# Retention's keys regrouped: 0 to 127, 128 to 255 and the last 16, in place of 16, 128 and 128

## The reference, cut to what matters

```
sc = jnp.einsum('bhid,bhjd->bhij', qc, kc) * intra          # decay gamma^|n-m|
o = (jnp.einsum('bhij,bhjv->bhiv', sc, vc)
     + jnp.einsum('bhid,bhdv->bhiv', qc * q_dec[:, :, None], S))
S = S * chunk_dec[:, None, None] + jnp.einsum('bhjd,bhjv->bhdv', kc * k_dec[:, :, None], vc)
```

## Time and profile before

| | |
|---|---|
| median of three runs | 1411.36 us (1410.07 to 1412.16) |
| the profiled execution | 1412.0 us, its span 1409.1 us |
| TensorE busy | 1385.0 us, 98% |
| VectorE, ScalarE, GpSimd busy | 1012.6, 697.2, 283.7 us |
| granted TensorE clock, mean | 0.996 |

### The profile page before, as it was taken

The page is one execution under the profiler, slowest core; times in us unless marked ns, Lnnn a source line. Parts: engine busy times, 40 slices in busy tenths (PEclk is TensorE's granted clock), DMA queues, the critical chain, the costliest instruction groups (busy, mean ns, idle before and its releaser), DMA issues.

```text
span 1409.1 us, 25044 instructions
## 1 busy us (share of the span) xinstructions
PE 1385.0 (98%) x10088; PEld 1321.5 (94%) x10088; DVE 1012.6 (72%) x1591; ACT 697.2 (49%) x1131; POOL 283.7 (20%) x273
## 2 busy tenths in 40 slices
PE   7999999999999999999999999999999999999997
PEld 7989999999999888889999999999999999888887
DVE  5668766655786988788666776766557785898864
ACT  5556544443654555544334564544444555555542
POOL 1014100022144100032244554000024402200021
PEclk9999999999999999999999999999999999999999
DMA  7424556655432755555444354555555552365552
GB/s 237 150 91 150 180 163 195 190 183 175 150 121 90 227 182 181 178 181 187 143 140 141 128 179 159 174 178 180 165 166 160 161 180 90 121 209 192 189 168 80
DMA packets 225482, 229.45 MB, mean 163 GB/s; under 512 B 13576, under 2 KB 218632, under 8 KB 225368
## 3 DMA queue, kind: packets, MB, share of 16 engines
q1 hardware_dynamic: 224432, 225.98, 49.9%
q10 hardware_dynamic: 936, 1.87, 0.6%
HBM read 226.51 MB, written 1.33 MB: 162 GB/s over the span
## 4 chain that ended last, share of the span: by engine, by line
PE 91%; DVE 5%; ACT 1%; issue 1%; POOL 0%; DMA 0%; POOLq 0%; DVEq 0%; ACTq 0%
PE ps L500 27%; PE ps L498 19%; PE ps L499 19%; PE ps L495 16%; DVE ul L1464 1%; PE ps L736 1%; PE ps L810 1%; PE ps L578 1%; PE ps L548 1%; PE ps L550 1%; PE ps L549 1%; PE ps L572 1%; PE ps L800 1%; PE ps L646 1%; PE ps L725 1%
## 5 line engine op out<-in xcount | busy, mean ns | idle before, releaser
L970 ACT ACTIVATE uh<-raw 128x1024 fp32r<-128x1024 f32 (+4 forms) x455 | 447.8, 993 | 466.7 <-PE ps L500 422.8
L1464 DVE TENSOR_TENSOR ul<-raw,uh 128x1024 fp32r<-128x1024 f32 (+4 forms) x455 | 534.2, 1180 | 141.5 <-PE ps L500 107.3
L500 PE MATMUL ps<-xx,ul 128*128 128x272 f32 (+1 forms) x2160 | 618.4, 286 | 0.0
L498 PE MATMUL ps<-xx,uh 128*128 128x272 f32 (+1 forms) x1456 | 430.3, 296 | 0.9 <-DVE ul L1464 0.8
L499 PE MATMUL ps<-xx,uh 128*128 128x272 f32 (+1 forms) x1456 | 418.6, 287 | 0.0
L500 PEld LDWEIGHTS ps<-xx,ul 128*128 128x128 f32 x2160 | 406.8, 188 | 0.1
L500 PE MATMUL ps<-aa,ul 128*128 128x272 f32 (+1 forms) x1104 | 315.4, 286 | 0.0
L498 PEld LDWEIGHTS ps<-xx,uh 128*128 128x128 f32 x1456 | 274.8, 189 | 5.3 <-issue 2.6
L499 PEld LDWEIGHTS ps<-xx,uh 128*128 128x128 f32 x1456 | 275.2, 189 | 1.2
L495 PE MATMUL ps<-xx,uh 128*128 128x512 f32 x704 | 248.5, 395 | 1.9 <-DVE ul L1464 1.1
L498 PE MATMUL ps<-aa,uh 128*128 128x272 f32 (+1 forms) x840 | 245.4, 292 | 2.9 <-ACT aa L1109 2.7
(11 more groups left out here) (256 smaller groups left out, 1386.4 us busy)
## 6 DMA issues: line engine op xcount, KB each, us to landing
raw<-in_ffn_w SPq DMA_DIRECT2D x60, 1024.0 KB, 5.2
raw<-in_ffn_w_in SPq DMA_DIRECT2D x44, 1024.0 KB, 5.2
raw<-in_ret_w_in SPq DMA_DIRECT2D x24, 1024.0 KB, 5.2
raw<-in_ffn_w_out SPq DMA_DIRECT2D x16, 1024.0 KB, 5.4
raw<-in_gla_w_in SPq DMA_DIRECT2D x12, 1024.0 KB, 5.6
raw<-in_ret_w_o SPq DMA_DIRECT2D x8, 1024.0 KB, 5.2
raw<-in_dsa_w_in SPq DMA_DIRECT2D x7, 1024.0 KB, 5.2
raw<-in_ffn_w_out SPq DMA_DIRECT2D x8, 768.0 KB, 4.9
```

What stands on the lines that cost most here:

```text
L498: e.matmul(ps[:, 0:n1 - n0], hi[:, k, :], x.hi[:, k0 + j, n0:n1], start=first and j == 0, stop=False)
L500: i = e.matmul(ps[:, 0:n1 - n0], lo[:, k, :], x.hi[:, k0 + j, n0:n1], start=False, stop=last and j == len(ks) - 1)
L970: i = e.activation(unit_hi(u)[:, :, cols], a, ACT.Copy)
L1464: i = e.tensor_tensor(unit_lo(u)[:, :, cols], a, unit_hi(u)[:, :, cols].bitcast(F32), ALU.subtract)
```

## The change

The 16 keys that stand alone move from the front to the end. The groups become keys 0 to 127 with 272 queries, 128 to 255 with the 192 queries from 80 on, and 256 to 271 with the 64 queries from 208 on. In all three kinds of matmul the small group is now taken at its true size: 16 stationary columns in the scores and the transposes, 16 stationary rows in the outputs. The second and third groups of scores share one bank and one step (r = 1), so that `scores` has two parts. VectorE multiplies them in two instructions. The memset and its semaphore fall away. The decay tables are 528 columns wide.

```diff
-NI = (272, 256, 128)
-I0 = (0, 16, 144)
-DOFF = (0, 272, 528)
-DW = 656
+RKEY = (0, 128, 256)
+RSIZE = (128, 128, 16)
+NI = (272, 192, 64)
+I0 = (0, 80, 208)
+DOFF = (0, 272, 464)
+DW = 528
...
             def ret_v(c):
-                to_tokens(("rv", c), tmp[4 + c % 2], *lin.emptied(("rv", c)))
-
-            def scores(hd, g):
-                ps = small(("rS", hd, g), "D")
+                ps = small(("rv", c), "A")
+                w.wait_ge(*lin.emptied(("rv", c)))
+                for g in range(3):
+                    i = e.transpose(ps[0:RSIZE[g], g * P:(g + 1) * P], tmp[4 + c % 2][:, RKEY[g]:RKEY[g] + RSIZE[g]], ident)
+                done(i, ("rv", c))
+
+            def scores(hd, part):
+
+                ps = small(("rS", hd, part), "D")
                 w.wait_ge(s_rrope, 4 * hd + 4)
-                for k in range(2):
-                    i = e.matmul(ps[:, 0:NI[g]], r_kq[:, 2 * hd + k, WIN[g]:WIN[g] + P], r_kq[:, 8 + 2 * hd + k, I0[g]:T],
-                                 start=(k == 0), stop=(k == 1))
-                done(i, ("rS", hd, g))
+                for g in (range(1), range(1, 3))[part]:
+                    to = ps[0:RSIZE[g], DOFF[g] - DOFF[part]:DOFF[g] - DOFF[part] + NI[g]]
+                    for k in range(2):
+                        i = e.matmul(to, r_kq[:, 2 * hd + k, RKEY[g]:RKEY[g] + RSIZE[g]], r_kq[:, 8 + 2 * hd + k, I0[g]:T],
+                                     start=(k == 0), stop=(k == 1))
+                done(i, ("rS", hd, part))
...
                 for g in range(3):
-                    i = e.matmul(ps[:, I0[g]:T], r_vt[:, g, c * P:(c + 1) * P], r_sc[hd % 2][:, DOFF[g]:DOFF[g] + NI[g]],
+                    keys = slice(0, RSIZE[g])
+                    i = e.matmul(ps[:, I0[g]:T], r_vt[keys, g, c * P:(c + 1) * P], r_sc[hd % 2][keys, DOFF[g]:DOFF[g] + NI[g]],
                                  start=(g == 0), stop=(g == 2))
...
-                    if r < 3:
+                    if r < 2:
                         scores(hd, r)
...
             def ret_v(c):
-                to_tokens(("rv", c), r_vt[:, :, c * P:(c + 1) * P], s_rzero, 1)
+                key, dst = ("rv", c), r_vt[:, :, c * P:(c + 1) * P]
+                ps = aux.bank(key)
+                w.wait_ge(*aux.full(key))
+                e.activation(dst[0:RSIZE[2], 2, :], ps[0:RSIZE[2], 2 * P:3 * P], ACT.Copy)
+                e.activation(dst[:, 0:2, :], ps[:, 0:2 * P].rearrange("p (a b) -> p a b", a=2), ACT.Copy).then_inc(
+                    aux.empties(key, "A"), 1)
...
-                        e.tensor_tensor(r_sc[hd % 2][:, cols], aux.bank(key)[:, 0:NI[r]], r_dk[hd % 2][:, cols],
-                                        ALU.mult).then_inc(aux.empties(key, "D"), 1)
+                        for g in (range(1), range(1, 3))[r]:
+                            cols, keys = slice(DOFF[g], DOFF[g] + NI[g]), slice(0, RSIZE[g])
+                            ps = aux.bank(key)[keys, DOFF[g] - DOFF[r]:DOFF[g] - DOFF[r] + NI[g]]
+                            i = e.tensor_tensor(r_sc[hd % 2][keys, cols], ps, r_dk[hd % 2][keys, cols], ALU.mult)
+                        i.then_inc(aux.empties(key, "D"), 1)
...
-            e.memset(r_vt[:, 0, :], 0.0).then_inc(s_rzero, 1)
```

More of the change, by code:

```diff
@@ L442, in build @@
                              "s_acc", "s_best", "s_mask", "s_bm", "s_dmax", "s_dexp", "s_drc", "s_dp", "s_dyh"))
-        (s_rstage, s_rzero, s_metah, s_metasq, s_metal, s_both, s_jr, s_rms, s_fin, s_rcs, s_rrope, s_rsum, s_rsub,
+        (s_rstage, s_metah, s_metasq, s_metal, s_both, s_jr, s_rms, s_fin, s_rcs, s_rrope, s_rsum, s_rsub,
          s_rsq, s_rinv, s_rO, s_rsilu, s_rmul, s_ryh, s_ryl) = (
-            sem(n) for n in ("s_rstage", "s_rzero", "s_metah", "s_metasq", "s_metal", "s_both", "s_jr", "s_rms", "s_fin", "s_rcs",
+            sem(n) for n in ("s_rstage", "s_metah", "s_metasq", "s_metal", "s_both", "s_jr", "s_rms", "s_fin", "s_rcs",
                              "s_rrope", "s_rsum", "s_rsub", "s_rsq", "s_rinv", "s_rO", "s_rsilu",
@@ L806, in ret_out @@
                 ps = small(("rO", c), "A")
-                w.wait_ge(*aux.emptied(("rS", hd, 2)))
+                w.wait_ge(*aux.emptied(("rS", hd, 1)))
                 w.wait_ge(*aux.emptied(("rv", c)))
                 for g in range(3):
-                    i = e.matmul(ps[:, I0[g]:T], r_vt[:, g, c * P:(c + 1) * P], r_sc[hd % 2][:, DOFF[g]:DOFF[g] + NI[g]],
+                    keys = slice(0, RSIZE[g])
+                    i = e.matmul(ps[:, I0[g]:T], r_vt[keys, g, c * P:(c + 1) * P], r_sc[hd % 2][keys, DOFF[g]:DOFF[g] + NI[g]],
                                  start=(g == 0), stop=(g == 2))
@@ L1324, in _ @@
                 if r == 0 and hd >= 2:
-                    w.wait_ge(*aux.emptied(("rS", hd - 2, 2)))
+                    w.wait_ge(*aux.emptied(("rS", hd - 2, 1)))
                     e.dma_start(r_dk[hd % 2], A["c_dec"][:, hd * DW:(hd + 1) * DW]).then_inc(s_dk[hd % 2], 16)
@@ L1926, in ret_after @@
                 if 0 <= hd < 4:
-                    if r < 3:
+                    if r < 2:
                         key = ("rS", hd, r)
-                        cols = slice(DOFF[r], DOFF[r] + NI[r])
                         w.wait_ge(*aux.full(key))
@@ L2362, in tables @@
     chunk = np.where(np.arange(T) < NM, 0, 1 + (np.arange(T) - NM) // 64)
-    size = (NM, P, P)
     for hd in range(4):
@@ L2366, in tables @@
         for w in range(3):
-            j = WIN[w] + np.arange(size[w])
+            j = RKEY[w] + np.arange(RSIZE[w])
             i = np.arange(I0[w], T)
@@ L2370, in tables @@
             m = np.where(chunk[j][:, None] <= chunk[i][None, :], m, 0.0)
-            dec[:size[w], hd, DOFF[w]:DOFF[w] + NI[w]] = m
+            dec[:RSIZE[w], hd, DOFF[w]:DOFF[w] + NI[w]] = m
     return tab, hot, dec.reshape(P, 4 * DW)
```

## The result

The changed kernel takes 1414.47 us (median of 12 runs, 1413.63 to 1416.59) against 1411.69 us for the kernel before (12 runs beside it): ratio 1.0022, 95% interval 1.0014 to 1.0030. It is slower by 2.8 us. That is the side that was forecast, but little more than a third of the size, +7.6, and close to what the rival "transposes keep their full width" gave, +2.9.

What follows compares the result with a forecast made beforehand. TensorE, without waits from 670 to 810 us, was taken as the bound; outputs +3.5, scores -0.6 and transposed values +4.7 summed to +7.6 us, 1419.0 us against the median; range 1413.0 to 1422.0, the forecast's own 1416.5 to 1420.5.

Steps and rivals of the forecast that it cites:

- transposes keep their full width: Rival: in the array transposes keep full width, plain matmuls don't, so only outputs and scores count: +2.9 us, 1414.3; chance 0.21.
- The bound: In retention, 670 to 810 us, only TensorE is waited for; array time added or removed should appear in the end time.
- The cost of a change of footing: On TensorE, each change to or from narrow operands costs 0.09 us emptying plus the next bare load, 0.104 for 128 columns.
- only fewer rows break the stream: Rival: on TensorE few stationary rows break the stream, few columns don't: +1.7 us, 1413.1; chance 0.10.
- Outputs, +3.5: 16 output matmul groups: narrower second group and 16-row third group with its breaks, net +0.22 us each, +3.5 in all.
- Scores, -0.6: Scores of 4 heads: fewer columns streamed, less the break for 16 stationary columns, net -0.16 us a head, -0.6 in all.
- Transposed values, +4.7: 16 third transposes of value chunks: 16 stationary columns break the stream, 0.40 us instead of 0.11, +4.7 in all.
- The two-record rival: Rival: the 16-column transpose runs as a two-record matmul besides breaking the stream: +9.3 us, 1420.7; chance 0.22.
- Behind TensorE, 0: Changes on VectorE, ScalarE, GpSimd and the decay loads are hidden behind the busy TensorE, so worth 0.
- Waits: In retention, with 12 banks a head instead of 13 and r = 2 gone, no wait comes late.
- The ends of the range: Whole-kernel time from the rows-only case, 1413.0 us, to the two-record case with outputs at their upper bound, 1422.0.

## Why the prediction failed, step by step

- *The bound*: right. TensorE stayed without holes through retention, and what was added to its stream came out at the end, +3.1 in the stage and +2.8 by the medians.
- *The cost of a change of footing*: right, for plain matmuls, for rows and for columns. The joint scores cost 1.18 us where no break would have made 0.65 + 0.22 = 0.87, so the rival "only fewer rows break the stream" falls too, and the time in the stage followed in every run that added such changes, halved their number or took them away.
- *Outputs, +3.5*: measured 8 x (2.69 - 2.23) = +3.7, or 2.69 for two where 2.67 was written.
- *Scores, -0.6*: measured 4 x (1.18 - 1.32) = -0.6.
- *Transposed values, +4.7*: **the step that failed.** Measured 0. I priced the transpose of 16 stationary columns like a plain matmul of such columns. It follows without a gap and in one record, three transposes in 0.33 us as before. The plain matmul in its place cost 0.41 us more in the chunk that was read, and, each against the kernel before beside it, 9.5 - 2.8 = 6.7 in all (expected 6.4), which shows that the fault was not the price but to what it applies. The rival was written down, with its time, 1414.3, and got 0.21 where the forecast had 0.38. I had no row for it, and the row of eight transposes with 16 rows, which do break the stream, made me take transposes to be like matmuls in columns too. Its operands have 16 rows and 16 columns, and since 16 columns alone don't break the stream, I put its gap down to the rows.
- *The two-record rival*: wrong for the same reason, and the experiment produced just that: two records and the break, +9.3 us forecast, 1420.71 - 1411.24 = +9.5 measured. The Trainium skill, TensorEngine Tiling (Array Packing), section Restrictions, excludes the transpose mode for fp32 data under column tiling. The trace agrees in so far as none of the 16 transposes of 128 rows by 16 columns showed a change of mode: each was one record, with no gap before or behind it. That they run in the full array is argued from this and not shown.
- *Behind TensorE, 0*: right. VectorE's products took 0.43, 0.34 and 0.20 us, and no wait arose.
- *Waits*: right, no new one; the run with the same banks and full widths was faster than before.
- *The ends of the range*: by the prediction's own terms they are 1413.1 and 1421.7 us; 1413.0 and 1422.0 are rounded outwards. Nothing hangs on it.

## What to carry over

In a stream of wide matmuls, padding a small fp32 operand to 128 by 128 can be the cheap form. Each change to few rows or few columns and each change back costs 0.09 us and lays the next load bare. Fewer rows save nothing for it: a record of 16 rows still loads 128 columns, and the padded kernel was the best in the stage, 115.3 us, against 118.2 with the narrow outputs in pairs, 117.9 before and 120.9 as changed. Fewer columns do save: a record of 64 moving columns takes 0.055 us with 16 stationary columns and 0.11 with 128. But four of them save 0.22, and the way in and out cost 0.31 (1.18 - 0.65 - 0.22). By these numbers six such records would have to stand behind each other before it pays; that is an estimate, and no run tried it. Regroup the work so that the padded group has the fewest moving columns, as the change did: with full widths this was 2.6 us better in the stage than the kernel before. And where a price was read from one kind of instruction, ask whether the trace shows it for the kind that it is put on.

## What the runs showed of the hardware that was not expected

- A PE transpose with 16 stationary columns (16 x 128 from 128 x 16, fp32) costs 0.11 us behind 128-wide ones and leaves no gap; a plain matmul of the same operands costs 0.41 us more, with its second record. The transposes of 16 rows by 16 columns do leave one, 0.36 us in the stream.
- For 16 rows by 128 columns and 64 moving columns, both records and the changes around them took 0.56 us; the same group padded to 128 rows, (2.02 - 1.57) / 2 = 0.22.
- One stretch of 3.4 us at the half clock, in the last layer's attention, appeared in one of two profiled executions of one program and not in the other.
